# Retention stage of a hybrid diffusion trunk: raw outputs kept in used key and query space, scores two items ahead, normalisation three items behind

## The reference

```python
def retention_out(o, g, gn_w, gn_b, w_out):
    mu = o.mean(-1, keepdims=True)
    var = jnp.square(o - mu).mean(-1, keepdims=True)
    o = (o - mu) * lax.rsqrt(var + LN_EPS)
    b, h, n, dv = o.shape
    o = o.transpose(0, 2, 1, 3).reshape(b, n, h * dv) * gn_w.astype(jnp.float32) + gn_b.astype(jnp.float32)
    return (o.astype(g.dtype) * jax.nn.silu(g)) @ w_out

y_ret = retention_out(bidir_retention(q_x, k_x, v_x, log_g, s_fwd, s_bwd), rg_x, ret_gn_w, ret_gn_b, ret_w_out)
y_fou = fourier_mix(fu_x) @ fou_w_out
```

## Time and profile before

| | us |
|---|---|
| median of 3 runs | 2575.18 |
| lowest, highest | 2574.51, 2578.59 |
| the profiled execution | 2576.9 |
| its span, first to last instruction | 2575.0 |

### The profile page before, as it was taken

One profiled execution on the slowest core, in us unless ns is written; L12 is line 12 of the kernel. 1 busy time (PEld: TensorE's weight loads), 2 busy tenths in 40 slices (PEclk: granted clock), 3 DMA queues, 4 the chain that ended last, 5 costly groups with the idle time before them and its releaser, 6 DMA issues.

```text
span 2575.0 us, 33634 instructions
## 1 busy us (share of the span) xinstructions
PE 2453.0 (95%) x13530; PEld 2120.2 (82%) x13530; DVE 1609.2 (62%) x2146; ACT 936.9 (36%) x1361; POOL 126.0 (5%) x163
## 2 busy tenths in 40 slices
PE   6999999997999999979999999999999899996998
PEld 6988988986876788869889888889888786995996
DVE  4566668756465544576666686666686554665655
ACT  2522355432114322244223554224554223443443
POOL 2000001000001000010000010000020001001000
PEclk9999999999999999989999999999999998997999
DMA  8455555651122343345455565455555242674763
GB/s 263 144 169 166 193 190 175 174 170 33 49 90 58 109 136 123 127 151 164 150 177 194 187 200 173 155 180 188 180 181 173 66 139 70 194 250 131 226 202 123
DMA packets 476814, 400.62 MB, mean 156 GB/s; under 512 B 36340, under 2 KB 428788, under 8 KB 476404
## 3 DMA queue, kind: packets, MB, share of 16 engines
q1 hardware_dynamic: 464992, 391.18, 47.9%
q10 hardware_dynamic: 11668, 7.30, 0.9%
HBM read 397.25 MB, written 1.17 MB: 155 GB/s over the span
## 4 chain that ended last, share of the span: by engine, by line
PE 87%; DVE 8%; ACT 3%; issue 2%; DMA 1%; ACTq 0%; SPq 0%; POOL 0%; POOLq 0%; DVEq 0%
PE ps L1327 25%; PE ps L1328 25%; PE ps L1329 25%; DVE wl L835 2%; PE ps L1585 2%; PE ps L1576 1%; PE ps L1597 1%; PE ps L1525 1%; ACT tB L524 1%; PE ps L1352 1%; ACT wh L506 1%; PE ps L1678 1%; DVE st L893 1%; PE ps L1359 1%; PE ps L1367 1%
## 5 line engine op out<-in xcount | busy, mean ns | idle before, releaser
L835 DVE TENSOR_TENSOR wl<-raw,wh 128x1024 fp32r<-128x1024 f32 x576 | 701.3, 1221 | 678.1 <-ACT wh L506 676.8
L506 ACT ACTIVATE wh<-raw 128x1024 fp32r<-128x1024 f32 x576 | 609.8, 1059 | 1290.1 <-PE ps L1329 1256.9
L1327 PE MATMUL ps<-hh,wh 128*128 128x256 f32 (+1 forms) x2736 | 897.0, 328 | 32.6 <-DVE hl L926 19.8
L1328 PE MATMUL ps<-hl,wh 128*128 128x256 f32 (+1 forms) x2736 | 889.0, 325 | 0.0
L1329 PE MATMUL ps<-hh,wl 128*128 128x256 f32 (+1 forms) x2736 | 888.8, 325 | 0.0
L1327 PEld LDWEIGHTS ps<-hh,wh 128*128 128x128 f32 x2736 | 525.2, 192 | 78.5 <-DVE hl L926 20.9
L1328 PEld LDWEIGHTS ps<-hl,wh 128*128 128x128 f32 x2736 | 525.2, 192 | 41.7 <-issue 1.0
L1329 PEld LDWEIGHTS ps<-hh,wl 128*128 128x128 f32 x2736 | 524.9, 192 | 41.2
L850 DVE SCALAR_TENSOR_TENSOR acc<-araw,c,acc 128x1024 f32<-128x1024 f32 x210 | 258.4, 1280 | 36.3 <-DMA araw<-in_ada_w 34.8
L1327 PE MATMUL ps<-wh,stage_h_f 128*128 128x512 f32 x616 | 240.8, 391 | 2.0 <-DVE stage_l_f L979 2.0
L1328 PE MATMUL ps<-wl,stage_h_f 128*128 128x512 f32 x616 | 239.7, 389 | 0.0
(11 more groups left out here) (160 smaller groups left out, 2388.8 us busy)
## 6 DMA issues: line engine op xcount, KB each, us to landing
raw<-in_ffa_w SPq DMA_DIRECT2D x204, 512.0 KB, 3.6
raw<-in_ffb_w SPq DMA_DIRECT2D x168, 512.0 KB, 3.9
raw<-in_mix_w_in SPq DMA_DIRECT2D x148, 512.0 KB, 4.0
araw<-in_ada_w SPq DMA_DIRECT2D x136, 512.0 KB, 5.1
raw<-in_mix_w_o SPq DMA_DIRECT2D x24, 512.0 KB, 4.3
raw<-in_ret_w_out SPq DMA_DIRECT2D x16, 512.0 KB, 4.0
raw<-in_na_fou_w_out SPq DMA_DIRECT2D x16, 512.0 KB, 3.9
raw<-in_ada_w SPq DMA_DIRECT2D x8, 512.0 KB, 5.2
```

Of the source, the lines that this page charges most:

```text
L506: A.activation(wh[:, s, :], raw[:, s, :], ACT.Copy).then_inc(w_rounded, 1)
L835: V.tensor_tensor(wl[:, s, :], raw[:, s, :], f(wh[:, s, :]), ALU.subtract).then_inc(w_split, 1)
L1327: T.matmul(out, a[0], b[0], start=start, stop=False)
L1328: T.matmul(out, a[0], b[1], start=False, stop=False)
```

## The change

The output of an item doesn't stay in PSUM until its factor is known. ACT, after the square, copies it (`r_raw`) into `kq`, into the columns of the keys and the queries of the same head and side, which no later scores read. The banks of the outputs go from three to two, and `values(t)` waits for `r_raw` of t-2 in place of `r_used` of t-3. The variance columns get bank 6, the spread block bank 7. The squares have two buffers. `rve` has four slots in place of two.

`spread(t)` no longer needs the diagonals: its stationary operand is the column of factors, read 128 times by a broadcast (step 0), and its moving operand the identity; it is two matmuls of 128 columns in place of one of 256. DVE's `diagonal`, the copy to `rsp` and `scale` are gone. `finish(t)` has four operations of 128 x 256: (spread block x weight x raw output) in place twice, then (+ bias) x gate twice.

The order: PE starts with scores(0) and scores(1), then for each t: values(t), scores(t+2), variance(t-1), spread(t-2). Behind the last item come form_a of `fu` 0, spread(last-1), variance(last), form_a of `fu` 1, spread(last). DVE, for each t: probs(t+1), dec_first, finish(t-3), variance(t-1), split. ACT does the exponentials ahead of the square and not behind it.

```diff
@@ ACT retention
-                for t in range(len(items)):
-                    act.wait_ge(r_out, b + t + 1)
-                    if t >= 1:
-                        act.wait_ge(r_var, b + t)
-                    A.activation(rq2[:], ps[:, 4 + t % 3].rearrange("p (a n) -> p a n", a=2), ACT.Square).then_inc(r_sq, 1)
+                for t, (h, s) in enumerate(items):
                     if t + 2 < len(items) and (t + 2) % per == 0 and (t + 2) // per >= early(l):
                         decay(l, (t + 2) // per)
+                    act.wait_ge(r_out, b + t + 1)
+                    if t >= 2:
+                        act.wait_ge(r_var, b + t - 1)
+                    y = ps[:, 4 + t % 2].rearrange("p (a n) -> p a n", a=2)
+                    A.activation(rq2[:, t % 2], y, ACT.Square).then_inc(r_sq, 1)
+                    A.copy(kq[:, h::4, s * SEQ:(s + 1) * SEQ], y).then_inc(r_raw, 1)
@@ DVE retention
-                def diagonal(t):
-
-                    dve.wait_ge(r_rstd, b + t + 1)
-                    for q in range(LT):
-                        ins = V.tensor_scalar(rr[:, t % 2, q], ident[:], rve[:, t % 2, q:q + 1], float(DV), ALU.mult, ALU.mult)
-                    ins.then_inc(r_diag, 1)
-
-                def scale(t):
+                    V.tensor_scalar(rve[:, t % 4], ps[:, 6, 0:LT], EPS, None, ALU.add).then_inc(r_vare, 1)
+
+                def finish(t):
+
+                    h, s = items[t]
+                    w = slice(s * SEQ, (s + 1) * SEQ)
                     dve.wait_ge(r_spread, b + t + 1)
-                    V.tensor_copy(rsp[:], ps[:, 7, 0:SEQ]).then_inc(r_taken, 1)
-                    dve.wait_ge(r_taken, b + t + 1)
-                    dve.wait_ge(r_sq, b + t + 1)
-                    for a in range(2):
-                        ins = V.tensor_tensor(ro[:, a], ps[:, 4 + t % 3, a * SEQ:(a + 1) * SEQ], rsp[:], ALU.mult)
-                    ins.then_inc(r_used, 1)
-                    dve.wait_ge(r_used, b + t + 1)
...
+                    dve.wait_ge(r_raw, b + t + 1)
                     for a in range(2):
                         k = 2 * h + a
-                        ins = V.tensor_scalar(ro[:, a], ro[:, a], gnw[:, l, k:k + 1], gnb[:, l, k:k + 1], ALU.mult, ALU.add)
-                    link(ins)
-                    w = rgz[:, 2 * h:2 * h + 2, s * SEQ:(s + 1) * SEQ]
-                    V.tensor_tensor(w, w, ro[:], ALU.mult).then_inc(r_fin, 1)
+                        ins = V.scalar_tensor_tensor(out=kq[:, 4 * a + h, w], in0=ps[:, 7, 0:SEQ], scalar=gnw[:, l, k:k + 1],
+                                                     in1=kq[:, 4 * a + h, w], op0=ALU.mult, op1=ALU.mult)
+                    ins.then_inc(r_taken, 1)
+                    dve.wait_ge(r_taken, b + t + 1)
+                    for a in range(2):
+                        k = 2 * h + a
+                        ins = V.scalar_tensor_tensor(out=rgz[:, k, w], in0=kq[:, 4 * a + h, w], scalar=gnb[:, l, k:k + 1],
+                                                     in1=rgz[:, k, w], op0=ALU.add, op1=ALU.mult)
+                    ins.then_inc(r_fin, 1)
...
-                for t in range(len(items) + 2):
-                    if t >= 2:
-                        scale(t - 2)
+                for t in range(len(items) + 3):
                     if t + 1 < len(items):
                         probs(t + 1)
+                    if t + 2 < len(items) and (t + 2) % per == 0 and (t + 2) // per >= early(l):
+                        dec_first(l, (t + 2) // per)
+                    if t >= 3:
+                        finish(t - 3)
                     if 1 <= t <= len(items):
                         variance(t - 1)
-                    if t >= 2:
-                        finish(t - 2)
-                    if 1 <= t <= len(items):
-                        diagonal(t - 1)
-                    if t + 2 < len(items) and (t + 2) % per == 0 and (t + 2) // per >= early(l):
-                        dec_first(l, (t + 2) // per)
@@ PE retention
-                    if t >= 3:
-                        pe.wait_ge(r_used, b + t - 2)
+                    if t >= 2:
+                        pe.wait_ge(r_raw, b + t - 1)
...
                 def spread(t):
 
-                    pe.wait_ge(r_diag, b + t + 1)
-                    T.matmul(ps[:, 7, 0:SEQ], mean256[:], rr[:, t % 2].rearrange("p q n -> p (q n)"), start=True, stop=True)\
-                     .then_inc(r_spread, 1)
+                    pe.wait_ge(r_rstd, b + t + 1)
+                    if t >= 1:
+                        pe.wait_ge(r_taken, b + t)
+                    for q in range(LT):
+                        ins = T.matmul(ps[:, 7, q * P:(q + 1) * P], rve[:, t % 4, q:q + 1].broadcast_to([P, P]), ident[:],
+                                       start=True, stop=True)
+                    ins.then_inc(r_spread, 1)
...
                 scores(0)
                 pe.wait_ge(rv_copied, NT * (l + 1))
-                for t in range(len(items) + 2):
-                    if t < len(items):
-                        values(t)
+                scores(1)
+                for t in range(len(items)):
+                    values(t)
+                    if t + 2 < len(items):
+                        scores(t + 2)
+                    if t >= 1:
+                        variance(t - 1)
                     if t >= 2:
                         spread(t - 2)
-                    if t + 1 < len(items):
-                        scores(t + 1)
-                    if 1 <= t <= len(items):
-                        variance(t - 1)
-                    if t == len(items):
-
-                        pe.wait_ge(r_prob, b + t)
-                        pe.wait_ge(in_copied, in0[l] + 1 + RET[l])
-                        form_a(AT["fu", l], 0, (hh, hl), mid(l))
+                last = len(items) - 1
+                pe.wait_ge(r_prob, b + last + 1)
+                pe.wait_ge(in_copied, in0[l] + 1 + RET[l])
+                form_a(AT["fu", l], 0, (hh, hl), mid(l))
+                spread(last - 1)
+                variance(last)
+                pe.wait_ge(in_copied, in0[l] + 1 + RET[l] + 1)
+                form_a(AT["fu", l] + 1, 1, (hh, hl), mid(l))
+                spread(last)
```

More of the change, by code:

```diff
@@ L148, in trunk @@
         vmean = sb("vmean", [P, 2, RH])
-        rvs = sb("rvs", [P, 4, LT])
-        rve, nhalf = rvs[:, 0:2], rvs[:, 2]
+        rvs = sb("rvs", [P, 36, LT])
+        rve, nhalf = rvs[:, 0:4], rvs[:, 4]
         nms = sb("nms", [P, 16])
@@ L237, in trunk @@
         dec_arg, dec_exp, dec_ready = sem("dec_arg"), sem("dec_exp"), sem("dec_ready")
-        rv_tile, nv_tile, r_score, r_prob, r_out, r_sq, r_var, r_vare, r_rstd, r_diag, r_spread, r_taken, r_used, r_fin = [
-            sem(n) for n in ("rv_tile", "nv_tile", "r_score", "r_prob", "r_out", "r_sq", "r_var", "r_vare", "r_rstd", "r_diag", "r_spread", "r_taken", "r_used", "r_fin")]
+        rv_tile, nv_tile, r_score, r_prob, r_out, r_sq, r_raw, r_var, r_vare, r_rstd, r_spread, r_taken, r_fin = [
+            sem(n) for n in ("rv_tile", "nv_tile", "r_score", "r_prob", "r_out", "r_sq", "r_raw", "r_var", "r_vare", "r_rstd", "r_spread", "r_taken", "r_fin")]
         f_one, f_onec, f_two, f_hi, f_lo = [sem(n) for n in ("f_one", "f_onec", "f_two", "f_hi", "f_lo")]
@@ L1654, in mixer @@
                 retention(l)
-                for j in range(1, 4):
+                for j in range(2, 4):
                     pe.wait_ge(in_copied, c0 + RET[l] + j)
```

21 lines of the change are left out of this document (9 added, 12 removed).

## The result

| | before | after |
|---|---|---|
| median of the runs, us | 2574.85 (4) | 2543.27 (4) |
| lowest, highest | 2570.2, 2578.59 | 2541.49, 2544.28 |
| profiled execution | 2576.9 | 2541.49 |
| its span | 2575.0 | 2539.7 |
| mean granted clock | 0.975 | 0.978 |

A forecast was written before the change was run, and what follows sets the result against it. PE, busy for 95% of the span, bounds the kernel, but this stage loses time to waits and half clock. Savings of 18.2 and 12.6 us, together 30.8, gave 2546.1 profiled and 2544.4 median; forecast 2544.5, range 2539 to 2554.

The forecast's parts named there:

- The sum: PE's work in the stage plus 1.66 us for the clock: 18.2 us saved in layer 0, 12.6 in layer 1.
- rival 1: The clock holds in layer 0 too, at the start: 1.66 us less, 2542.7; chance 0.15.
- Scores two ahead: scores(t+2) behind values(t) on PE give DVE a whole turn; slack some 0.9 us in layer 0, 3 in layer 1.
- Normalisation three behind: finish(t-3) on DVE frees the spread's bank 3.9 us after DVE's release, against some 4.0 on PE: close, but holds.
- DVE's load: finish priced at 1.52 us per item; DVE 6.1 us against PE's 6.7 in layer 1, its saving worth nothing by itself.
- ACT's copy: One more 128 x 512 operation from PSUM on ACT, 0.59 us: hidden; uncovered it would be 7 us.
- The new spread: Four 128-column records on PE with a step-0 stationary operand: 0.55 us taken, 0.43 from below, 1.1 from above.
- Two banks in place of three cost nothing: Fewer output banks cost nothing, as values(t+2) want the copy of t, done a whole turn earlier.
- The tail: Behind the last item, form_a 1 covers POOL's power and finish(last-1); DVE is back on time for unit 3.
- the ring: The stage before: scores(t+1) late on PE, then DVE's backlog, then values(t+1); 8.8 us of waits for `rp`.
- Rival 2: A wait is left in each item as DVE's slacks go: 2551 with slow weights, 2561 with 1.4 us each; chance 0.18.
- Rivals 3 and 4: Clock falls for the whole stage, 38 us slower, 2614, chance 0.05; nothing comes of the change, 2575, chance 0.05.

The follow-up runs named there:

- probs first: The kernel before with one change on DVE, probs(t+1) ahead of scale(t-2): 2595.55 us, ratio 1.0082.
- scores late: The changed kernel with scores(t+1) behind values(t), as before the change, and scores(1) not issued at the start: 2565.39 us, ratio 0.996.
- gap at the start: The changed kernel with scores(1) moved from ahead of values(0) to behind it: 2551.61 us, ratio 0.9907.
- the old operations: The changed kernel's order, banks, raw copies and lag, with DVE's operations of before and one 256-column spread matmul: 2549.1 us, ratio 0.9884.
- both orders: The kernel before with scores two ahead on PE and probs ahead of scale on DVE, nothing else: 2577.47 us, ratio 1.0012.
- scores ahead alone: The kernel before with scores(1) issued at the start and scores(t+2) in place of scores(t+1): 2582.6 us, ratio 1.0026.
- the last kernel: The changed kernel with head 0's decay sum earlier, fu 3's copy ahead of the fourth split, splits ahead of finish: 2534.75 us, ratio 0.9838.

## Why the prediction was right, and where it wasn't

**The sum.** It priced the stage as PE's work without a gap, and PE's work without a gap it became. Layer 0, from values(0) to the second form_a, took 628.56 - 583.65 = 44.91 us, against 45.19 of work in the sum; layer 1 took 2017.97 - 1992.90 = 25.07, against 25.58. Form_a of `fu` 0 starts 38.08 us behind values(0) in layer 0 (38.4 + 1.7 was named) and 20.86 in layer 1 (21.3). The gain over the stage, 20.3 + 13.2 = 33.5 us, is 2.7 above the forecast's 30.8, for two reasons. (The medians of the whole time differ by 31.6.) 1.66 is the half clock at values(0) of layer 0, which the forecast kept and the profiled execution didn't have: rival 1 came true in it. The other 1.0 are small rates, on the safe side: values behind a spread take 3.46 us (603.18 to 606.64) for 3.56, variance 0.81 (597.60 to 598.41) for 0.85, and the 0.12 for the last spread of each layer was covered. "PE's work is hardly less, what goes is waiting" holds for the records and not for their time: 14.6 of the 33.5 us are shorter records, most of it half clock that is gone.

**Rival 1 is settled for that execution and not in general.** Behind one gap of 3.00 us values(0) fell to half clock in 8 of 8 layer starts (before, probs first, scores late, gap at the start). Behind the smaller gaps of the new start they did so in 2 of 20 (the other ten traced executions), and both are among the eight starts with the gaps of 1.05 and 0.73 us in a row, all of layer 0. The forecast kept the loss, which was the less likely case; it costs 1.7 us.

**Scores two ahead.** The mechanism was told wrongly. "Scores(t+1) come late on PE" isn't what held values back: with the scores early and nothing else, the wait stayed at 1.66 us. But the step's estimate of the new order, a slack on DVE of some 0.9 us in layer 0, holds: probs(4) are 1.45 us early, and the experiment with late scores shows what the step protects, 19 us.

**Normalisation three behind.** "Close, but it holds; where it fails PE waits tenths": PE waited 0.19 us, twice, for `r_taken`. The turn with s = 1 is 4.24 us (598.94 to 603.18) for 4.0, that with s = 0 6.60 (592.34 to 598.94) for 6.7.

**DVE's load.** `finish` takes 1.70 us (0.90 + 0.80, from 601.65 to 603.35) for 1.52: its operations have two inputs and a scalar, and were priced by a pair with two inputs and none. "Its saving is worth nothing by itself" holds nearly: the old operations in the new order cost 1 to 3 us of the stage.

**ACT's copy.** 578 ns is the mean of the 8 of layer 0 in the trace of after, 0.59 us was taken; no wait on PE names it.

**The new spread.** 0.53 us (598.41 to 598.94), 0.55 was taken, from the row of another stage. But it isn't dearer than the old one by the 0.12 that the prediction takes. The 0.43 of the old one is read where scores follow it. Where variance stands ahead of it and values behind it, the old spread takes 0.52, too (602.24 to 602.76; timeline of PE, 594 to 614 us of the kernel with the old operations, in which values are L1524):

```profile
602.24 0.68 PE L1544 MATMUL ps<-rr,mean 128*128 128x256 f32 x2
602.76 1.89 PE L1524 MATMUL ps<-rp,rv 128*128 128x256 f32 x8
```

And the new one takes 0.45 where variance follows it (627.30 to 627.75) and 0.36 to 0.45 ahead of form_a. So the start-to-start price of so short a group depends on its neighbours. By the figure for a weight load in the Trainium skill (TensorE: Matmul & The Clock Gate, LDWEIGHTS) the spread was to be 0.43; the trace agrees ahead of variance (0.45) and for records with one column (0.81 us for 8, 0.101 each), and has 0.1 more ahead of values.

**"Two banks in place of three cost nothing."** True as a cost, but the move of the banks got no term as a benefit. With the variance columns back in bank 7 the change loses 5.3 us, and in the old kernel with both orders PE's waits stand ahead of writes into that bank, in a stage as long as before. That a bank of its own would be enough there was not tried. Someone who followed the prediction's story and changed only the order would have got nothing (2577.47 beside 2575.3).

**The tail.** "form_a 1 covers POOL's power and finish(last-1)": it does, and uncovered it is 2.8 us a layer in the traced execution. The prediction gave the tail no term of its own in its story of the ring, but it is 13.9 of the 33.5 us. In before PE waited there for the diagonals (2.09 us ahead of 642.05) and for the copy (0.61 ahead of 643.36), and variance and the first records of form_a ran at half clock behind.

**Rival 2, a wait in each item,** was the nearest danger. POOL's power takes 0.69 to 0.96 us when DVE does other things, but 1.60 us beside DVE's split, as in layer 0 (timeline of POOL, 580 to 640 us of after):

```profile
598.83 1.61 POOL L804 TENSOR_TENSOR rvs<-rvs 128x2 f32<-128x2 f32 x1 [5.11 <-DVE rvs L1084]
603.58 0.95 POOL L804 TENSOR_TENSOR rvs<-rvs 128x2 f32<-128x2 f32 x1 [3.15 <-DVE rvs L1084]
```

It used up 0.8 us that the accounts of slack had not got, and there was room for it: spread wants it a whole turn later. Rivals 3 and 4 (a stage at half clock, nothing) are refuted by the clock of 1.00 and by the gain.

**What stays open.** Several things changed together between "both orders" (138.1) and the change with the old operations (108.7): the raw copies, which free the output bank without the factor; the spread and its DVE work an item later; the bank of its own; the spread behind variance and not ahead of it on PE; ACT's exponentials ahead of the square, for which DVE had waited 0.79 us in "both orders"; and the new tail. The 29.4 us between them lie half in the middle (15.6) and half in the tail (15.5), while a half clock at the start takes 1.7 back. Two prices are known, both in the new order: the bank of its own, 5.3 us, and the third item of lag, 1.8. How the rest is shared out is not shown. The raw copies can't be taken out alone: with two output banks that are freed by the scaling, values(t) on PE would wait for a spread that stands behind it on PE.

## What to carry to other kernels

When a wait is found, walk the ring on which it lies back to where it began, and ask of every link what it would wait for if the present reason were gone; here three rings lay behind one another, and the edits that opened one or two of them shortened the stage by no more than 1.1 us or lengthened it by 10. A PSUM bank into which PE writes while another engine must first read its neighbour columns is such a link: count how many items lie between. If the stage is then dense on the engine that bounds it, the sum of its groups, start to start at full clock, gives its new length; here it was within 1% in layer 0 and 2% in layer 1.

## What the runs showed of the hardware

**The clock fell behind gaps of about 1 us, and not every time.** It fell behind 1.14 us in the tail (0.72 in the 6 us from 636), behind 1.66 us in the middle, and in two executions of eight behind gaps of 1.05 and 0.73 us in a row. Within one execution, that with the scores late, the spread and values(4) were slow behind a gap of 1.46 us (1.19 and 4.83 us long), and the next such pair, spread and values(6), ran at full speed behind one of 1.47 (0.68 and 3.62). In the kernel with scores ahead alone the waits of 1.66 us for `rp` in the middle were those of before, but one more stretch of 6 us ran at half clock: of the 3.2 us by which its period grew, 2.6 are the clock, and a comparison of waits alone would have missed them. The Trainium skill (TensorE: Matmul & The Clock Gate, "Why this matters for your kernels") names only longer gaps as a cause; the rows differ, and the measurement decides.

**POOL beside DVE.** The power of 128 x 2 values took 1.60 to 1.63 us three times in each layer, each time beside the split (L835, two inputs from SBUF). In the last kernel, with the splits elsewhere, the longest in layer 0 was 1.07, and the one power that still ran beside a split, in layer 1, took 1.61. The Trainium skill (GPSIMD Engine Reference, Specifications, the row on SBUF interfaces) names DVE instructions with two SBUF inputs as a cause of such contention, which agrees.
